# Reciprocal sums of two attentions written 64 columns wide and turned by two transposes a group

## What is computed

```python
def block(qi):                                    # one block of 128 queries
    sc = jnp.einsum('bhgqd,bhkd->bhgqk', qi, kh)  # scores against 512 keys
    p = jax.nn.softmax(sc, axis=-1)
    return jnp.einsum('bhgqk,bhkd->bhgqd', p, vh)
```

```python
p = jax.nn.softmax(jnp.concatenate([s_win, s_ctx], axis=-1), axis=-1)
return (jnp.einsum('bhwrc,brwchd->bwhd', p_win, v_win)
        + jnp.einsum('bhwl,blhd->bwhd', p_ctx, vc))
```

## Time and profile before

| | us |
|---|---|
| median of 3 runs | 1786.76 |
| lowest and highest | 1785.47 to 1789.37 |
| the profiled execution, whole | 1785.14 |
| its span in the trace | 1783.4 |
| PE busy | 1665.0 (93%) |
| DVE busy | 590.9 (33%) |
| ACT busy | 461.1 (26%) |
| POOL busy | 240.3 (13%) |

### The profile page before, as it was taken

The page is one execution under the profiler, slowest core; times in us unless marked ns, Lnnn a source line. Parts: engine busy times, 40 slices in busy tenths (PEclk is TensorE's granted clock), DMA queues, the critical chain, the costliest instruction groups (busy, mean ns, idle before and its releaser), DMA issues.

```text
span 1783.4 us, 21389 instructions
## 1 busy us (share of the span) xinstructions
PE 1665.0 (93%) x8797; PEld 966.9 (54%) x8797; DVE 590.9 (33%) x1070; ACT 461.1 (26%) x888; POOL 240.3 (13%) x116
## 2 busy tenths in 40 slices
PE   8999999999999979979889899899899999999998
PEld 6897686643434324333233243333376558878886
DVE  4997784541210202102002020010076461260074
ACT  5367725410000000000000000000075533353242
POOL 0004512000000000000000000000030674116330
PEclk9999999999999999999999999999999999999999
DMA  9344055389999999999999999999930105212121
GB/s 345 138 133 131 1 166 230 146 331 428 428 427 427 428 428 428 429 428 429 428 428 428 429 428 428 428 420 428 418 115 4 45 12 119 95 35 106 55 101 47
DMA packets 67733, 486.06 MB, mean 273 GB/s; under 512 B 10348, under 2 KB 20037, under 8 KB 41935
## 3 DMA queue, kind: packets, MB, share of 16 engines
q1 hardware_dynamic: 67663, 485.06, 67.2%
HBM read 482.64 MB, written 2.41 MB: 272 GB/s over the span
## 4 chain that ended last, share of the span: by engine, by line
PE 70%; DMA 22%; DVE 4%; issue 2%; ACT 2%; POOL 0%; POOLq 0%; ACTq 0%; SPq 0%; DVEq 0%
PE psum L598 20%; DMA ring<-in_expert_w_gu 13%; PE psum L2077 12%; PE psum L2162 9%; DMA ring<-in_expert_w_down 8%; PE psum L2060 3%; PE psum L2176 3%; PE psum L1654 2%; PE psum L3230 2%; PE psum L761 2%; PE psum L2906 2%; PE psum L739 2%; PE psum L726 2%; PE psum L2921 1%; PE psum L1789 1%
## 5 line engine op out<-in xcount | busy, mean ns | idle before, releaser
L2077 PE MATMUL psum<-ring,work_area 128*64 128x512 f32 x2048 | 455.3, 596 | 52.7 <-DMA ring<-in_expert_w_gu 52.4
L2077 PEld LDWEIGHTS psum<-ring,work_area 128*64 128x64 f32 x2048 | 142.3, 137 | 346.6 <-issue 251.3
L2162 PE MATMUL psum<-ring,work_area 128*64 128x512 f32 x1008 | 228.2, 600 | 8.8 <-DMA ring<-in_expert_w_down 6.8
L2280 DVE TENSOR_TENSOR work_area<-psum,work_area 128x512 f32<-128x512 f32 x32 | 20.6, 686 | 593.9 <-ACT work_area L2220 593.9
L2220 ACT ACTIVATE work_area<-psum 128x512 f32<-128x512 f32 x32 | 17.4, 594 | 523.0 <-PE psum L2077 523.0
L2162 PEld LDWEIGHTS psum<-ring,work_area 128*64 128x64 f32 x1008 | 73.1, 137 | 136.4 <-issue 120.5
L2478 POOL TENSOR_TENSOR hn<-x_res,extra 128x1024 f32<-128x1024 f32 x2 | 4.7, 2376 | 863.8 <-DVE x_res L2291 863.8
L2358 POOL TENSOR_TENSOR block_lo<-ring,part_hi 128x1024 fp32r<-128x1024 f32 x35 | 84.6, 2427 | 159.7 <-ACT part_hi L2351 159.3
L598 PE MATMUL psum<-h_hi,part_hi 128*128 128x512 f32 x240 | 93.7, 390 | 1.0 <-DVE hn L882 1.0
L598 PE MATMUL psum<-h_hi,block_lo 128*128 128x512 f32 x240 | 93.4, 389 | 0.0
L598 PE MATMUL psum<-h_lo,part_hi 128*128 128x512 f32 x240 | 93.4, 389 | 0.0
(11 more groups left out here) (536 smaller groups left out, 2745.5 us busy)
## 6 DMA issues: line engine op xcount, KB each, us to landing
ring<-in_expert_w_gu SPq DMA_DIRECT2D x128, 2048.0 KB, 31.6
ring<-in_expert_w_down SPq DMA_DIRECT2D x63, 2048.0 KB, 28.4
ring<-in_w_in SPq DMA_DIRECT2D x12, 2048.0 KB, 7.9
extra<-in_w_mod SPq DMA_DIRECT2D x4, 1536.0 KB, 10.5
ring<-in_w_out SPq DMA_DIRECT2D x3, 2048.0 KB, 12.5
hn<-in_w_mod SPq DMA_DIRECT2D x2, 1536.0 KB, 6.6
ring<-in_ca_wkv SPq DMA_DIRECT2D x2, 1024.0 KB, 8.2
x_res<-in_x SPq DMA_DIRECT2D x2, 1024.0 KB, 12.3
```

Source lines behind the costliest of these rows:

```text
L2077: ins = pe.matmul(psum[h * 64:(h + 1) * 64, c, :], xsT[:, k, e * CAP:(e + 1) * CAP], w[:, (2 * c + h) * BANK:(2 * c + h + 1) * BANK], star ...
L2162: ins = pe.matmul(psum[n * 64:(n + 1) * 64, 6, :], hidT[b][:, j, h, :], w[:, j, n * BANK:(n + 1) * BANK], start=(q == 0 and j == 0), stop= ...
```

## The change

`attention` gets an argument `wide`, a tile of 2 x 256 columns: in the first attention columns 3072 to 3583 of `x_res`, in the third columns 8704 to 9215 of `work_area`. `recips` writes the reciprocals of a group there, each 64 times over (its input is the four sums with a repeated last dimension), so the instruction goes from 128x4 to 128x256 elements. `out_pe` then transposes the tile in two pieces of 128x128 (two units each) where it had four products. The cross attention does not take this path. There are 8 groups in each of the two attentions, 16 in all.

```diff
+            wide_recip = lambda n: wide[:, n % 2 * T * dv:(n % 2 + 1) * T * dv]
...
                     pe.wait_ge(sem("at_recip"), recips_done + n + 1)
-                    for u in range(T):
-                        q, j = u // nj, u % nj
-                        pe.matmul(B.at(g)[j * dv:(j + 1) * dv, cols + q * P:cols + (q + 1) * P],
-                                  group_recip(n)[:, u:u + 1].to_broadcast([P, dv]), ident, start=True, stop=True,
-                                  skip_group_check=True)
+                    for q in range(T // nj):
+                        pe.transpose(B.at(g)[:, cols + q * P:cols + (q + 1) * P],
+                                     wide_recip(n)[:, q * nj * dv:(q + 1) * nj * dv], ident)
...
                     dve.wait_ge(exped, exped_before + (n + 1) * T)
-                    dve.reciprocal(group_recip(n), group_sums(n)).then_inc(sem("at_recip"), 1)
+                    dve.reciprocal(wide_recip(n).rearrange("p (u d) -> p u d", u=T),
+                                   group_sums(n).unsqueeze(2).to_broadcast([P, T, dv])).then_inc(sem("at_recip"), 1)
...
-            scaled_out(lambda i, q: by_rows(ymixT[:, 4 + i, :], q.start // GRID_W, q.stop // GRID_W), False), step=2,
+            scaled_out(lambda i, q: by_rows(ymixT[:, 4 + i, :], q.start // GRID_W, q.stop // GRID_W), False), step=2, wide=x_flat[:, 3 * D:3 * D + 2 * T * HD],
...
-            scaled_out(lambda i, q: obT[:, i, SHIFT + q.start:SHIFT + q.stop], True), step=2, bias=na_bias,
+            scaled_out(lambda i, q: obT[:, i, SHIFT + q.start:SHIFT + q.stop], True), step=2, bias=na_bias, wide=W[:, 8704:8704 + 2 * T * HD],
```

More of the change, by code:

```diff
@@ L662, in attention @@
         def attention(heads, width, qk_at, v_at, dv, pbuf, ptbuf, o_out, step=1, late=True, turners=(act, dve), bias=None,
-                      turned_from=None, besides={}, outs=None, before_last_out=None, o_later=O_LATER, o_behind=(0, 0)):
+                      turned_from=None, besides={}, outs=None, before_last_out=None, o_later=O_LATER, o_behind=(0, 0), wide=None):
             nkt, np_ = width // P, len(pbuf)
```

## The result

| | before | changed |
|---|---|---|
| median of the runs, us | 1786.74 (1785.47 to 1789.37) | 1806.82 (1804.84 to 1810.37) |
| ratio | | 1.0113, 95% interval 1.0099 to 1.0126 |
| span of the profiled execution | 1783.4 | 1806.4 |
| mean granted clock of the profiled execution | 0.997 | 0.993 |
| DVE busy | 590.9 | 615.0 |

The change makes the kernel 20.1 us slower. The forecast was 1800.5 with a range up to 1805.0, so the sign and the wait behind the loss held. The size did not: one term was too small and another, the clock, was left out of the sum.

A forecast was written before the change was run, and what follows sets the result against it. The prediction took PE's chain to bound both attentions before, and the path through DVE's long reciprocal after. Delays of 7.2 and 6.5 us, together 13.7, on the median of 1786.76 gave 1800.5 us, range 1793.0 to 1805.0.

The forecast's parts named there:

- The price of the reciprocal: DVE's reciprocal of 256 columns in both attentions takes 1753 ns, 1.58 us more in each of 16 groups.
- PE waits in every group, the loop through DVE becomes the bound: In both attentions PE waits for the reciprocal in all 16 groups; first-attention period 7.2 us instead of 6.30.
- The delay reaches the end: Both attentions' delays, 7.2 and 6.5 us, are passed on in full, the first one through the experts.
- The lag: From the reciprocal's start to the same group's L881 in both attentions: 2.73 + 1.58 - 0.23 = 4.08 us.
- The clock: Rival: longer PE waits in each attention's last group cost clock, 1.75 us each, giving 1803.9 us; chance 0.07.
- The argument from the experts' share of idle time: Against all groups losing clock (28 us): the experts had PE idle 13 of 100 us at clock 1.00.
- The prediction's own sign: The forecast is wrong if the granted clock of 169 to 230, at the first attention, is under 0.98.
- The sum: Group delays of both attentions: 7.2 and 6.5 us, together 13.7; 12.1 with the larger saving, 17.6 with the longer reciprocal.
- The range: For the whole kernel's time: 1793.0 us (swallowed delay) to 1805.0 us (sum's upper bound with one cold stretch).
- cheap reciprocal: Rival: the wide reciprocal takes only 0.35 us in both attentions, PE stays the bound, 1783.4 us; chance 0.06.
- swallowed by the experts: Rival: the experts' weight stream hides the first attention's delay, only 6.5 us left, 1793.3 us; chance 0.07.
- slower a column: Rival: the long reciprocal in both attentions costs 7.25 ns a column, 1.99 us, giving 1804.3 us; chance 0.04.

The follow-up runs named there:

- experiment 2: The change in the first attention alone, the neighbourhood attention left as in the kernel before: 1797.89 us, ratio 1.0066.
- experiment 1's second run: The changed kernel with the wide reciprocal kept, but four plain products as before instead of the two transposes: 1810.05 us, ratio 1.0129.
- experiment 1: Here its first run: the changed kernel with a narrow reciprocal widened by a 128x256 copy, both transposes kept: 1786.02 us, ratio 0.9997.
- experiment 3: The changed kernel with unneeded products ahead of PE's wait: two a group, six in the last, 1814.38 us; repeated with one and three, 1801.9 us.

## Why the prediction failed on the size

- **The price of the reciprocal** held: 1.753 us expected, 1.740 and 1.743 measured in the two attentions. The slope of the shorter ones carried to 256 columns.
- **PE waits in every group, the loop through DVE becomes the bound** held: 16 waits, 0.79 to 1.03 us each in 14 groups. The last waits were 3.1 and 2.7 us; the prediction had said 3.1 for both, since it took the old wait of 1.56 us for both attentions, and in the second it was 1.2. Period 7.29, expected 7.2.
- **The delay reaches the end** held: experiment 2 shows it.
- **The lag** was mis-sized: 4.08 expected, 4.22 measured. The step that failed is "so 0.26 for two. Saved: 0.23 us of PE time a group", put into the lag. The 0.26 were eight transposes in a row divided by four, but here two stand between a wait and a product of another kind: the trace after gives 186.16 - 185.82 = 0.34 from the first transpose to the first product, 0.08 more. The products' 0.49 were read where PE does not wait; behind a wait they take 0.46 (experiment 1's second run: 193.02 to 193.48), 0.03 less, and the 2.73 us of the last group held them at that length already. The last 0.03 are the time from the first values' product to L881, 1.99 against 1.96 in the last group before. So the saving is 0.12, and 0.09 by the lags of the two runs. In a stage that PE bounds it is 0.21 (experiment 1): the 0.23 nearly held for the old stage, and the forecast carried it over into the new one. 16 x 0.14 = 2.2 us.
- **The clock** was the step that cost most. The prediction priced it, at 1.75 us for each last wait on top of the same sum, but gave it a chance of 0.07 and left it out of the 1800.5. It came at both last waits, dearer in the first attention (2.7 us, 1.6 in the other), and at a third place (1.5 us) that I had taken for safe, since 13% of idle time among the experts had cost nothing. By experiment 3 it is 4.9 us, by the trace 5.8: the values' products of the fifth group; the spread, the values' products and the transposes behind them in the last group; the values' products of the neighbourhood attention's last group. The argument from the experts' share of idle time was the weak one. The trace before had a cold stretch behind much shorter waits: the two ahead of the earlier trace rows were 0.33 and 0.64 us, both for DVE (the prediction says DVE and ACT). The prediction's own sign, a clock under 0.98 at 169 to 230, did come: 0.97. Which waits bring the clock down is not shown; that filling them keeps it up is.
- **The sum again:** 13.7 + 2.2 + 5.8 = 21.7 of 23.0 us of span. The other 1.2 us lie outside the attentions: 0.45 less at the start, 1.2 won back ahead of the experts, 0.8 lost in them, and the 2.0 behind them. Without the clock, 13.7 + 2.2 = 15.9 stands against the 16.1 us of experiment 3. Cold stretches differ from run to run: the changed kernel took 1804.84 us at a mean clock of 0.995 and 1810.37 at 0.991, and the wait ahead of the one at 1380 to 1390 brought one in four traces of nine.
- **The range** does not follow from the prediction's own numbers. Its upper end is said to be the upper bound of the sum with one cold stretch; that is 1786.76 + 17.6 + 1.75 = 1806.1, not 1805.0, and it still misses the 1806.82. With both last waits cold it is 1807.9 and would have held the time, but only by the longer reciprocal in it, which did not come.

The rivals "cheap reciprocal" (1.74 measured), "swallowed by the experts" (experiment 2) and "slower a column" (6.2 ns) are refuted.

## What to carry to other kernels

Ask of an instruction that grows whether somebody waits for its end, not whether its engine has idle time: the same 1.7 us cost 20 us ahead of the hand-over and 1 or 2 behind it. Compute the reciprocal on as few columns as there are results, and repeat it with something cheap. When a change makes PE wait where it did not, price the clock along with the wait, on top of the forecast and not as an alternative to it.

## What the runs showed of the hardware

- A reciprocal on DVE takes 6.2 ns a column up to 256 columns, repeated inputs included (1.74 us), where a reduction of 256 columns from SBUF took 0.42 and a copy 0.29.
- A 128x256 copy from SBUF to SBUF took 1.55 and 1.52 us when it ran into a GpSimd instruction. Beside the same work the 128x256 reciprocal took its 1.74 us, the 128x256 reduction its 0.42 and the 128x512 copy out of PSUM its 0.68.
- The granted clock fell to 1.2 GHz behind waits of 3.1 and 2.7 us, and behind two of 1.26 and 1.03 with 0.63 us of work between, while behind two of 0.93 to 0.97 and 1.03 in the seventh group, with the same work between, it fell in one trace (experiment 1's second run) and not in two (the changed kernel, experiment 2). Behind one and the same wait of 1.92 us it fell in four of nine traces. Waits of 1.03 every 7.3 us left it at 2.4 GHz. Filling 0.86 us of each wait with unneeded products (2.7 in the last groups) kept it up in both attentions, and the kernel was 4.9 us faster.
